# Two row norms moved into the output projections in front of them, with the projection's second half of columns taken by blocks of rows

## The chip, the cores and the metric

The kernel runs on one core of one Trainium2 chip. The metric is the device time of one execution in microseconds (us). A core has five engines with queues of their own: PE (TensorE, matrix products; "PEld" is its weight load), DVE (VectorE), ACT (ScalarE), POOL (GpSimd) and SP (SyncE, which here only issues transfers, DMAs). They are ordered among each other by semaphores alone.

## The reference

A block of one hybrid layer (a delta-rule branch and a sparse attention branch) is followed by two layers of a second model, the first with a dense feed-forward part and the second with eight experts. The sequence has 1024 tokens, the model width is 1024, everything is float32. What the change touches:

```
# end of the first block                      # layer 0 of the second block
y = concat([y_rwkv, y_attn]) @ w_out          x = x + concat([a, r]) @ w_out[0]
x = x + y                                     h = rmsnorm(x, ffn_norm[0])
x = rmsnorm(x, final_g)                       x = x + swiglu(h, dense weights)
                                              # layer 1: the same mix, then experts
rmsnorm(x, g) = x * rsqrt(mean(x*x, axis=-1) + 1e-6) * g
```

## The kernel before

The kernel is a sequence of stages. Each stage opens its own on-chip tiles and semaphores, runs one block of instructions per engine, and ends with `Stage.end`, which clears the semaphores and holds all engines at a barrier. So no work of one stage overlaps work of the next. Between stages activations are either on chip or in device memory: `x_block` (result of the first block), `x_mixed0` (after the mixing half of layer 0), `h_rows` (normed rows for the feed-forward part).

A float32 product is made of three products of rounded parts: a tile is rounded on ACT into a `high` part, DVE subtracts that from the tile for the `low` part, and PE adds high x high, high x low and low x high into one accumulator.

`product_rows` is the output projection, run three times (first block, layer 0, layer 1). Its operand is the transposed mix `lhsT`, 8 tiles (`k`) of 128 x 1024, its weights are 1024 x 1024. The outer loop is the half of the columns (`h`, 512 columns), then `k`, then the eight blocks `b` of 128 rows, one PSUM bank for each block. One step `n = 8h + k` loads one weight tile of 128 x 512 (256 KB, L1618), rounds operand tile and weight tile (ACT, L1657 and L1658), splits them (DVE, L1665 and L1666) and gives PE 24 products of 512 columns (L1639). All of these tiles have two buffers, so ACT rounds step n only when PE has finished step n-2, and the operand is rounded and split again in the second half. The residual rows come in two transfers of 2 MB (L1621), each issued on SP right behind a half's first weight tile. When a half's last `k` is done, DVE adds each bank to the residual (L1682). With `out` given (the two layers) SP then writes the rows (L1625).

`norm_rows` is the row norm in a stage of its own. The sequence is: all eight sums of squares on ACT (L1717, over 1024 columns), one mean for the eight blocks (DVE, L1725), one root (ACT, L1720), one reciprocal (DVE, L1727), eight scalings by root and gain (DVE, L1731), each written by SP (L1707), and then the wait for the last write. In the first block (`block_norm`) the rows are on chip from the projection. In layer 0 (`ffn_norm`, called by `dense_ffn`) they are read back from `x_mixed0` first (L1702). Behind `block_norm` stands `norm_transpose` of layer 0 (`mix_norm0`, its first load is L183), behind `ffn_norm` stands `swiglu_passes` (first weight load L2692 on SP, first rows `h_rows` on POOL, L2736).

## Time and profile before

| | |
|---|---|
| median of 3 runs | 5874.25 us (5873.77 to 5884.84) |
| the profiled execution, its own time | 5870.24 us |
| its span | 5868.6 us |
| PE busy | 5236.5 us (89% of the span) |
| DVE, ACT, POOL busy | 2812.8, 2150.8, 380.2 us (48%, 37%, 6%) |
| mean granted clock of PE | 0.94 of full speed |
| moved by DMA | 697.32 MB, 119 GB/s on average |

PE is the busiest engine in nearly every stretch of the run, so what a stage costs is mostly its products; where the row of PE has a hole, another engine or a transfer sets the time. A page of the profile gives busy shares for the whole run only. The time around the two norms has to be read from the timeline, engine by engine, since there PE does nothing at all and the stages are separated by barriers.

### The profile page before, as it was taken

How to read it: one execution, taken by the hardware profiler on the slowest of the kernel's cores; microseconds unless marked ns; L12 is line 12 of the kernel's file. 1: busy time of each engine (PE TensorE's matmuls, PEld its weight loads, DVE VectorE, ACT ScalarE, POOL GpSimd, SP SyncE). 2: the span in 40 equal slices, each digit the busy share in tenths (PEclk: the TensorE clock that was granted, in tenths of full speed). 3: DMA queues.
4: the chain of work that ended last, by engine and by line, in shares of the span. 5: the costliest groups of instructions: out<-in, count | busy, mean ns of one | idle time of the engine just before them, and what ended most of it. 6: DMA issues, size and time to landing. Idle time of an engine off the chain costs nothing. (4 is left out here: it accounts for less than half of the span.)

```text
span 5868.6 us, 96708 instructions
## 1 busy us (share of the span) xinstructions
PE 5236.5 (89%) x38308; PEld 4564.4 (78%) x38309; DVE 2812.8 (48%) x4375; ACT 2150.8 (37%) x3178; POOL 380.2 (6%) x577
## 2 busy tenths in 40 slices
PE   6984778969899599999799996999999999999994
PEld 5663776758776499999677775989898999999994
DVE  2598334451563355555228434444444555555444
ACT  2212114432344244444324432333333444444432
POOL 0113000000230000000005001000000000000001
PEclk8995999979999799999899996999999999999997
DMA  1110000031000555554210414444444455555544
GB/s 70 50 58 16 2 2 35 28 116 43 19 18 24 210 188 209 204 205 161 79 38 2 135 63 165 166 167 151 156 160 157 183 194 187 189 193 189 181 157 181
DMA packets 109898, 697.32 MB, mean 119 GB/s; under 512 B 12592, under 2 KB 16448, under 8 KB 68544
## 3 DMA queue, kind: packets, MB, share of 16 engines
q1 hardware_dynamic: 95744, 647.08, 30.5%
q0 software_dynamic: 9088, 28.48, 1.4%
q10 hardware_dynamic: 4800, 17.83, 0.8%
q8 instruction: 213, 3.49, 0.2%
q14 instruction: 53, 0.43, 0.0%
HBM read 631.06 MB, written 62.29 MB: 118 GB/s over the span
## 5 line engine op out<-in xcount | busy, mean ns | idle before, releaser
L3255 DVE TENSOR_TENSOR experts_low<-experts_raw,experts_high 128x1024 fp32r<-128x1024 f32 x678 | 810.7, 1224 | 1001.2 <-ACT experts_high L3184 1001.1
L3119 PE MATMUL ps<-experts_xs_high,experts_high 128*128 128x256 f32 (+1 forms) x3584 | 1038.2, 290 | 33.9 <-issue 32.5
L3119 PE MATMUL ps<-experts_xs_high,experts_low 128*128 128x256 f32 (+1 forms) x3584 | 1040.5, 290 | 0.0
L3119 PE MATMUL ps<-experts_xs_low,experts_high 128*128 128x256 f32 (+1 forms) x3584 | 1038.8, 290 | 0.0
L3119 PEld LDWEIGHTS ps<-experts_xs_high,experts_high 128*128 128x128 f32 x3584 | 680.3, 190 | 46.5 <-issue 37.1
L3184 ACT ACTIVATE experts_high<-experts_raw 128x1024 fp32r<-128x1024 f32 x678 | 687.8, 1049 | 36.6 <-DMA experts_raw<-experts 36.6
L3119 PEld LDWEIGHTS ps<-experts_xs_low,experts_high 128*128 128x128 f32 x3584 | 680.8, 190 | 9.1
L3119 PEld LDWEIGHTS ps<-experts_xs_high,experts_low 128*128 128x128 f32 x3584 | 680.8, 190 | 0.0
L2794 PE MATMUL ps<-dense_xs_parts,dense_high 128*128 128x256 f32 x2816 | 499.2, 280 | 4.2 <-DVE dense_xs_parts L2897 2.7
L2794 PEld LDWEIGHTS ps<-dense_xs_parts,dense_high 128*128 128x128 f32 x2816 | 436.6, 189 | 12.5 <-issue 5.0
L3111 PE MATMUL ps<-experts_high,experts_hid_high 128*128 128x512 f32 x1120 | 444.7, 397 | 0.0
L3111 PE MATMUL ps<-experts_low,experts_hid_high 128*128 128x512 f32 x1120 | 441.9, 395 | 0.0
L2794 PE MATMUL ps<-dense_xs_parts,dense_low 128*128 128x256 f32 x1408 | 393.7, 280 | 0.0
L3208 ACT ACTIVATE experts_silu<-ps 128x288 f32<-128x288 f32 (+1 forms) x224 | 89.1, 398 | 807.1 <-PE ps L3119 807.1
L2903 DVE TENSOR_TENSOR dense_low<-dense_raw,dense_high 128x1024 fp32r<-128x1024 f32 x270 | 323.3, 1222 | 65.3 <-ACT dense_high L2832 65.3
L3111 PE MATMUL ps<-experts_high,experts_hid_low 128*128 128x512 f32 x896 | 354.1, 395 | 0.0
L2832 ACT ACTIVATE dense_high<-dense_raw 128x1024 fp32r<-128x1024 f32 x270 | 283.8, 1054 | 55.9 <-PE ps L2779 22.4
L2794 PEld LDWEIGHTS ps<-dense_xs_parts,dense_low 128*128 128x128 f32 x1408 | 265.6, 189 | 0.0
L3214 ACT ACTIVATE experts_hid_high<-experts_hid 128x288 fp32r<-128x288 f32 (+1 forms) x224 | 96.6, 431 | 408.9 <-DVE experts_hid L3273 408.9
L3111 PEld LDWEIGHTS ps<-experts_low,experts_hid_high 128*128 128x128 f32 x1120 | 210.5, 188 | 39.9
L3111 PEld LDWEIGHTS ps<-experts_high,experts_hid_high 128*128 128x128 f32 x1120 | 210.4, 188 | 39.8
L3111 PEld LDWEIGHTS ps<-experts_high,experts_hid_low 128*128 128x128 f32 x896 | 168.3, 188 | 41.1
(547 smaller groups left out, 9144.1 us busy)
## 6 DMA issues: line engine op xcount, KB each, us to landing
experts_raw<-experts SPq DMA_DIRECT2D x226, 1536.0 KB, 6.3
dense_raw<-dense SPq DMA_DIRECT2D x90, 1536.0 KB, 6.3
mixT<-w_in SPq DMA_DIRECT2D x36, 512.0 KB, 3.2
y_slot<-mla_blank SPq DMA_DIRECT2D x15, 1152.0 KB, 20.7
out_proj_raw<-w_out SPq DMA_DIRECT2D x48, 256.0 KB, 2.7
proj_keys_raw<-w_in SPq DMA_DIRECT2D x20, 512.0 KB, 3.3
x_mixed<-x_out SPq DMA_DIRECT2D x16, 512.0 KB, 4.7
y_slot<-experts_y ACTq DMA_DIRECT2D x8, 1024.0 KB, 8.7
```

Source lines behind the costliest of these rows:

```text
L2794: last = nc.tensor.matmul(bank(u, m, SLOTS), w[:, u, m, c], x[:, k, :], start=(k == 0 and i == 0), stop=(k == KD - 1 and i == 2))
L2832: nc.scalar.activation(high[:, v, t, :], raw[:, v, t, :], ACT.Copy).then_inc(rounded, 1)
L2903: nc.vector.tensor_tensor(low[:, v, t, :], raw[:, v, t, :], high[:, v, t, :].bitcast(F32), ALU.subtract).then_inc(split, 1)
L3111: last = nc.tensor.matmul(ps[:, 2 + 2 * a + h, :], x, w[:, v, 2, c], start=first and i == 0, stop=last_one and i == len(terms) - 1)
L3119: last = nc.tensor.matmul(ps[:, m, 0:width], w[:, u, m, c], x[:, k, 0:width], start=(k == 0 and i == 0), stop=(k == KD - 1 and i == 2))
L3184: nc.scalar.activation(high[:, v, t, :], raw[:, v % NR, t, :], ACT.Copy).then_inc(rounded, 1)
L3208: nc.scalar.activation(silu[:, u % 2, 0:width], ps[:, 0, 0:width], ACT.Silu).then_inc(silu_done, 1)
L3214: nc.scalar.activation(hid_high[:, u % 2, 0:width], hid[:, u % 2, 0:width], ACT.Copy).then_inc(hid_rounded, 1)
L3255: nc.vector.tensor_tensor(low[:, v, t, :], raw[:, v % NR, t, :], high[:, v, t, :].bitcast(F32), ALU.subtract).then_inc(split, 1)
```

## The change

A new stage function, `product_and_norm`, takes the place of `product_rows` and `norm_rows` in the first block, and of `product_rows` in layer 0 together with `norm_rows` in `dense_ffn`. `norm_rows` is gone. Layer 1 keeps `product_rows`.

In the new stage the high and low parts of the operand (`x_high`, `x_low`) and of the weights have eight slots, one for each `k`. The operand is rounded and split once, in the first half. The first half of the columns runs as before, `k` outside and the eight blocks inside. During it the weight tiles of the second half are loaded and split into the slots that PE has finished with. The residual (and later the result) lies in the operand's own memory, so its one transfer of 4 MB waits until all eight operand tiles are split; SP issues it behind the tenth weight tile. The second half runs block by block: the 24 products of block 0, then of block 1, and so on, in the banks 0, 1 and 7 in turn. Behind each block's products DVE adds the bank to the rows, ACT sums the squares of the second half of the row (those of the first half were summed between the halves), DVE makes the mean, ACT the root, DVE the reciprocal and the scaled row, and SP writes it, while PE goes on with the next blocks. In layer 0 SP also writes the unscaled rows to `x_mixed0`, ahead of the scaled ones, and scaled rows have two buffers of their own. In the first block `masks` and in layer 0 `down` and `z` are released before the stage, which makes room.

```diff
--- before.py
+++ after.py
@@ -1683,53 +1683,142 @@
     st.end()
 
 
-def norm_rows(core, name, x, gain_row, out=None, source=None):
+def product_and_norm(core, name, xT, weights, source, gain_row, normed, out=None):
+
+
+
 
 
     nc = core.nc
     st = Stage(core, name)
-    junk = st.sb("junk", [P, D])
-    stat = st.sb("stat", [P, 3, NT])
+    K = 8
+    BANKS = (0, 1, 7)
+    x = as_rows(xT)
+    raw = st.sb("raw", [P, 2, HALF])
+    high = st.sb("high", [P, K, HALF], F32R)
+    low = st.sb("low", [P, K, HALF], F32R)
+    x_high = st.sb("x_high", [P, K, T], F32R)
+    x_low = st.sb("x_low", [P, K, T], F32R)
     gain = st.sb("gain", [P, D])
-    x_loaded = [st.sem(f"x_loaded{b}") for b in range(NT)]
-    loaded, summed, mean, root, inverse, normed, written = (
-        st.sem(n) for n in ("loaded", "summed", "mean", "root", "inverse", "normed", "written"))
+    junk = st.sb("junk", [P, HALF])
+    stat = st.sb("stat", [P, 6, NT])
+    rows = None if out is None else st.sb("rows", [P, 2, D])
+    row = lambda b: x[:, b, :] if out is None else rows[:, b % 2, :]
+    loaded = [st.sem(f"loaded{i}") for i in range(2)]
+    stored = [st.sem(f"stored{i}") for i in range(2)]
+    (xin, gain_in, rounded, split, used, product, added, summed, eased, mean, root, inverse, scaled, written) = (
+        st.sem(n) for n in ("xin", "gain_in", "rounded", "split", "used", "product", "added", "summed", "eased", "mean", "root",
+                            "inverse", "scaled", "written"))
     with nc.Block(name) as block:
         @block.sync
         def _(sp):
-            if source is not None:
+            for n in range(2 * K):
+                h, k = divmod(n, K)
+                if n >= 2:
+                    sp.wait_ge(split, n - 1)
+                sp.dma_start(raw[:, n % 2, :], weights[k * P:(k + 1) * P, h * HALF:(h + 1) * HALF]).then_inc(loaded[n % 2], 16)
+                if n == 1:
+                    sp.dma_start(gain[:, :], gain_row.to_broadcast([P, D])).then_inc(gain_in, 16)
+                if n == K + 1:
+                    sp.dma_start(x, source.rearrange("(b p) n -> p b n", p=P)).then_inc(xin, 16)
+            for b in range(NT):
+                if out is not None:
+                    sp.wait_ge(added, NT + b + 1)
+                    sp.dma_start(out[b * P:(b + 1) * P, :], x[:, b, :]).then_inc(written, 16)
+                sp.wait_ge(scaled, b + 1)
+                sp.dma_start(normed[b * P:(b + 1) * P, :], row(b)).then_inc(stored[b % 2], 16)
+            if out is not None:
+                sp.wait_ge(written, 16 * NT)
+            for i in range(2):
+                sp.wait_ge(stored[i], 16 * NT // 2)
+
+        @block.tensor
+        def _(pe):
+            def three(bank, k, b):
+                c = slice(b * P, (b + 1) * P)
+                nc.tensor.matmul(core.ps[:, bank, :], x_high[:, k, c], high[:, k, :], start=(k == 0), stop=False)
+                nc.tensor.matmul(core.ps[:, bank, :], x_high[:, k, c], low[:, k, :], start=False, stop=False)
+                return nc.tensor.matmul(core.ps[:, bank, :], x_low[:, k, c], high[:, k, :], start=False, stop=(k == K - 1))
+
+            for k in range(K):
+                pe.wait_ge(split, k + 1)
                 for b in range(NT):
-                    sp.dma_start(x[:, b, :], source[b * P:(b + 1) * P, :]).then_inc(x_loaded[b], 16)
-            sp.dma_start(gain[:, :], gain_row.to_broadcast([P, D])).then_inc(loaded, 16)
-            if out is not None:
-                for b in range(NT):
-                    sp.wait_ge(normed, b + 1)
-                    sp.dma_start(out[b * P:(b + 1) * P, :], x[:, b, :]).then_inc(written, 16)
-                sp.wait_ge(written, 16 * NT)
+                    last = three(b, k, b)
+                    if k == K - 1:
+                        last.then_inc(product, 1)
+                if k < K - 1:
+                    last.then_inc(used, 1)
+            for b in range(NT):
+                if b < 3:
+                    pe.wait_ge(added, BANKS[b] + 1)
+                else:
+                    pe.wait_ge(added, NT + b - 2)
+                for k in range(K):
+                    if b == 0:
+                        pe.wait_ge(split, K + k + 1)
+                    last = three(BANKS[b % 3], k, b)
+                last.then_inc(product, 1)
 
         @block.scalar
         def _(act):
+            def square(h, b):
+                act.wait_ge(added, h * NT + b + 1)
+                if h or b:
+                    act.wait_ge(summed, h * NT + b)
+                nc.scalar.activation(junk[:, :], x[:, b, h * HALF:(h + 1) * HALF], ACT.Square,
+                                     accum_out=stat[:, h, b:b + 1]).then_inc(summed, 1)
+
+            for n in range(2 * K):
+                h, k = divmod(n, K)
+                act.wait_ge(loaded[n % 2], 16 * (n // 2 + 1))
+                if h == 0:
+                    nc.scalar.activation(x_high[:, k, :], xT[:, k, :], ACT.Copy)
+                elif k < K - 1:
+                    act.wait_ge(used, k + 1)
+                else:
+                    act.wait_ge(product, NT)
+                nc.scalar.activation(high[:, k, :], raw[:, n % 2, :], ACT.Copy).then_inc(rounded, 1)
             for b in range(NT):
-                if source is not None:
-                    act.wait_ge(x_loaded[b], 16)
-                if b:
-                    act.wait_ge(summed, b)
-                nc.scalar.activation(junk[:, :], x[:, b, :], ACT.Square,
-                                     accum_out=stat[:, 0, b:b + 1]).then_inc(summed, 1)
-            act.wait_ge(mean, 1)
-            nc.scalar.activation(stat[:, 2, :], stat[:, 1, :], ACT.Sqrt).then_inc(root, 1)
+                square(0, b)
+            for b in range(NT):
+                square(1, b)
+                act.wait_ge(mean, b + 1)
+                nc.scalar.activation(stat[:, 4, b:b + 1], stat[:, 3, b:b + 1], ACT.Sqrt).then_inc(root, 1)
 
         @block.vector
         def _(dve):
+            def split_step(n):
+                dve.wait_ge(rounded, n + 1)
+                if n < K:
+                    nc.vector.tensor_tensor(x_low[:, n, :], xT[:, n, :], x_high[:, n, :].bitcast(F32), ALU.subtract)
+                nc.vector.tensor_tensor(low[:, n % K, :], raw[:, n % 2, :], high[:, n % K, :].bitcast(F32), ALU.subtract)\
+                    .then_inc(split, 1)
+
+            def add(h, b):
+                dve.wait_ge(product, h * NT + b + 1)
+                xs = x[:, b, h * HALF:(h + 1) * HALF]
+                nc.vector.tensor_tensor(xs, xs, core.ps[:, BANKS[b % 3] if h else b, :], ALU.add).then_inc(added, 1)
+            for n in range(2 * K - 1):
+                split_step(n)
+            dve.wait_ge(xin, 16)
+            for b in range(NT):
+                add(0, b)
+            split_step(2 * K - 1)
             dve.wait_ge(summed, NT)
-            nc.vector.tensor_scalar(stat[:, 1, :], stat[:, 0, :], 1.0 / D, 1e-6, ALU.mult, ALU.add).then_inc(mean, 1)
-            dve.wait_ge(root, 1)
-            nc.vector.reciprocal(stat[:, 0, :], stat[:, 2, :]).then_inc(inverse, 1)
-            dve.wait_ge(inverse, 1)
-            dve.wait_ge(loaded, 16)
+            nc.vector.tensor_scalar(stat[:, 2, :], stat[:, 0, :], 1.0 / D, 1e-6, ALU.mult, ALU.add).then_inc(eased, 1)
+            dve.wait_ge(eased, 1)
+            dve.wait_ge(gain_in, 16)
             for b in range(NT):
-                nc.vector.scalar_tensor_tensor(x[:, b, :], x[:, b, :], stat[:, 0, b:b + 1], gain[:, :],
-                                               ALU.mult, ALU.mult).then_inc(normed, 1)
+                add(1, b)
+                dve.wait_ge(summed, NT + b + 1)
+                nc.vector.scalar_tensor_tensor(stat[:, 3, b:b + 1], stat[:, 1, b:b + 1], 1.0 / D, stat[:, 2, b:b + 1], ALU.mult, ALU.add)\
+                    .then_inc(mean, 1)
+                dve.wait_ge(root, b + 1)
+                nc.vector.reciprocal(stat[:, 5, b:b + 1], stat[:, 4, b:b + 1]).then_inc(inverse, 1)
+                dve.wait_ge(inverse, b + 1)
+                if out is not None and b >= 2:
+                    dve.wait_ge(stored[b % 2], 16 * (b // 2))
+                nc.vector.scalar_tensor_tensor(row(b), x[:, b, :], stat[:, 5, b:b + 1], gain[:, :], ALU.mult, ALU.mult).then_inc(scaled, 1)
     st.end()
 
 
@@ -3390,8 +3479,6 @@
 def dense_ffn(core, source, out):
 
     nc, d = core.nc, core.dram
-    with nc.sbuf_tensor("ffn_x", [P, NT, D], F32) as x:
-        norm_rows(core, "ffn_norm", x, d["dense_g"], d["h_rows"], source)
     swiglu_passes(core, "dense", DFF // P, d["dense"], out, residual=source)
 
 
@@ -3421,8 +3508,8 @@
     with ExitStack() as s1:
         sb = lambda name, shape: s1.enter_context(nc.sbuf_tensor(f"{name}{l}", shape, F32))
         mixT = sb("mixT", [P, 8, T])
-        down = sb("down", [P, 6, T])
-        z = sb("z", [P, 4, T])
+        rest = s1.enter_context(ExitStack())
+        down, z = (rest.enter_context(nc.sbuf_tensor(f"{name}{l}", [P, n, T], F32)) for name, n in (("down", 6), ("z", 4)))
         with ExitStack() as s2:
             sb2 = lambda name, shape: s2.enter_context(nc.sbuf_tensor(f"{name}{l}", shape, F32))
             qk = sb2("qk", [P, 2, 4, T])
@@ -3453,8 +3540,12 @@
                                     (down[:, n, b * P:(b + 1) * P], key_rope[:, :])],
                       lambda n, j: values[:, j, n * P:(n + 1) * P],
                       lambda b: core.c("causal")[:, T - (b + 1) * P:T], 192 ** -0.5, mixT[:, 0:4, :], fill=l == 1)
+        rest.close()
         if dump:
             dump(core, f"mix{l}", mixT[:, :, :].rearrange("p a n -> p (a n)"))
+        if l == 0:
+            product_and_norm(core, f"out_proj{l}", mixT[:, :, :], d[f"w_out{l}"], source, d["dense_g"], d["h_rows"], out)
+            return
         x = sb("x_out", [P, NT, D])
         product_rows(core, f"out_proj{l}", mixT, 8, d[f"w_out{l}"], 2, x, source, out)
 
@@ -3466,9 +3557,9 @@
 
 def first_block(core, dump):
     nc, d = core.nc, core.dram
-    with nc.sbuf_tensor("masks", [P, offset(NT) - offset(TOPK // P)], F32) as masks:
-        with nc.sbuf_tensor("big", [P, 5, 4, T], F32) as big, nc.sbuf_tensor("small", [P, T], F32) as small:
-            flat = big[:, :, :, :].rearrange("p a j n -> p (a j) n")
+    with nc.sbuf_tensor("big", [P, 5, 4, T], F32) as big:
+        flat = big[:, :, :, :].rearrange("p a j n -> p (a j) n")
+        with nc.sbuf_tensor("masks", [P, offset(NT) - offset(TOPK // P)], F32) as masks, nc.sbuf_tensor("small", [P, T], F32) as small:
             down, queries, relu = flat[:, 0:4, :], flat[:, 8:10, :], flat[:, 10:12, :]
             with nc.sbuf_tensor("index_weight", [P, NT, IDX_HEADS], F32) as weight, ExitStack() as s2:
                 xT = split_tensors(core, s2, "xT", [P, KD, T])
@@ -3502,13 +3593,11 @@
                     pair_products(core, "values_up", lambda n: flat[:, 4 + n, :],
                                   [[(w_uv[:, 2 * r, :], o_lat[:, 2 * r, :]), (w_uv[:, 2 * r + 1, :], o_lat[:, 2 * r + 1, :])]
                                    for r in range(4)], gate=lambda n: space[:, n, :])
-            if dump:
-                dump(core, "mixT", flat[:, 0:8, :].rearrange("p a n -> p (a n)"))
-            with nc.sbuf_tensor("x_res", [P, NT, D], F32) as x:
-                product_rows(core, "out_proj", flat[:, 0:8, :], 8, d["w_out"], 2, x, d["x"])
-                norm_rows(core, "block_norm", x, d["final_g"], d["x_block"])
-                if dump:
-                    dump(core, "x1", x[:, :, :].rearrange("p a n -> p (a n)"))
+        if dump:
+            dump(core, "mixT", flat[:, 0:8, :].rearrange("p a n -> p (a n)"))
+        product_and_norm(core, "out_proj", flat[:, 0:8, :], d["w_out"], d["x"], d["final_g"], d["x_block"])
+        if dump:
+            dump(core, "x1", flat[:, 0:8, :].rearrange("p a n -> p (a n)"))
 
 
 def index_weights(core, small, weight):
```

## Rows read from the trace of the kernel before

**Rows 1.** The page's first part: busy time and share of the span of each engine.
```profile
PE 5236.5 (89%) x38308; PEld 4564.4 (78%) x38309; DVE 2812.8 (48%) x4375; ACT 2150.8 (37%) x3178; POOL 380.2 (6%) x577
```

**Rows 2.** Timeline of PE behind both norms: start, us, instructions [idle before <-releaser].
```profile
1273.93 5.01 PE L270 MATMUL ps<-cst,mixT 128*128 128x128 f32 x24 [36.33 <-DVE mixT L235]
...
2036.00 1.97 PE L2761 MATMUL ps<-cst,dense_xs 128*128 128x128 f32 x8 [54.49 <-DMA dense_xs<-h_rows]
```

**Rows 3.** Timeline of DVE, ACT and SP from the first block's projection to the next stage.
```profile
1232.96 5.37 DVE L1682 TENSOR_TENSOR x_res<-x_res,ps 128x512 f32<-128x512 f32 x8 [2.70 <-PE ps L1639]
...
1248.50 1.28 ACT L1720 ACT_TABLE_LOAD   x1
...
1250.27 9.66 DVE L1731 SCALAR_TENSOR_TENSOR x_res<-x_res,block_norm_stat,block_norm_gain 128x1024 f32<-128x1024 f32 x8
...
1264.18 0.32 SPq L183 DMA_DIRECT2D qk<-x_block  x1
```

**Rows 4.** The same from layer 0's projection to the dense stage.
```profile
1976.86 5.37 DVE L1682 TENSOR_TENSOR x_out<-x_out,ps 128x512 f32<-128x512 f32 x8 [2.70 <-PE ps L1639]
...
2005.84 9.66 DVE L1731 SCALAR_TENSOR_TENSOR ffn_x<-ffn_x,ffn_norm_stat,ffn_norm_gain 128x1024 f32<-128x1024 f32 x8
...
2019.72 37.97 SPq L2692 DMA_DIRECT2D dense_raw<-dense  x7
```

**Rows 5.** Instructions on single tiles: duration in ns min/median/max, first and last start.
```profile
L1682 DVE TENSOR_TENSOR x_res<-x_res,ps x16: 679/684/689, 1191.5 to 1237.6; 128x512 f32<-128x512 f32 x16
L1731 DVE SCALAR_TENSOR_TENSOR x_res<-x_res,block_norm_stat,block_norm_gain x8: 1280/1281/1285, 1250.3 to 1258.6; 128x1024 f32<-128x1024 f32 x8
L1658 ACT ACTIVATE out_proj_high<-out_proj_raw x48: 612/613/617, 1145.1 to 3514.1; 128x512 fp32r<-128x512 f32 x48
```

**Rows 6.** Timeline of ACT and DVE in `norm_transpose`, where squares and roots alternate.
```profile
1272.17 0.19 ACT L203 ACTIVATE mix_norm_stat<-mix_norm_stat 128x1 f32<-128x1 f32 x1
1272.38 1.06 ACT L199 ACTIVATE mixT<-qk 128x1024 f32<-128x1024 f32 x1
1273.35 0.19 ACT L199 ACTIVATION_READ_ACCUMULATOR mixT<-qk 128x1 f32 x1
1273.44 0.19 ACT L203 ACTIVATE mix_norm_stat<-mix_norm_stat 128x1 f32<-128x1 f32 x1
...
1272.30 0.15 DVE L223 TENSOR_SCALAR mix_norm_stat<-mix_norm_stat 128x1 f32<-128x1 f32 x1 [3.25 <-ACT mixT L199]
1272.39 0.17 DVE L227 RECIPROCAL mix_norm_stat<-mix_norm_stat 128x1 f32<-128x1 f32 x1
```

**Rows 7.** Timeline of ACT: two successive steps, each released by PE's products.
```profile
1205.06 1.06 ACT L1657 ACTIVATE out_proj_x_high<-big 128x1024 fp32r<-128x1024 f32 x1 [3.86 <-PE ps L1639]
1210.50 1.06 ACT L1657 ACTIVATE out_proj_x_high<-big 128x1024 fp32r<-128x1024 f32 x1 [3.86 <-PE ps L1639]
```

**Rows 8.** Timeline of PE between the two halves of the first block's projection.
```profile
1192.88 0.39 PE L1639 MATMUL ps<-out_proj_low,out_proj_x_high 128*128 128x512 f32 x1
1193.11 0.39 PE L1639 MATMUL ps<-out_proj_high,out_proj_x_low 128*128 128x512 f32 x1
1193.80 0.47 PE L1639 MATMUL ps<-out_proj_high,out_proj_x_high 128*128 128x512 f32 x1 [0.30 <-PE ps L1639]
```

**Rows 9.** Timeline of PE: products at the lower clock, then from one bank to the next at the higher.
```profile
1149.04 0.63 PE L1639 MATMUL ps<-out_proj_high,out_proj_x_high 128*128 128x512 f32 x1
1149.46 0.63 PE L1639 MATMUL ps<-out_proj_low,out_proj_x_high 128*128 128x512 f32 x1
...
1152.99 0.39 PE L1639 MATMUL ps<-out_proj_high,out_proj_x_low 128*128 128x512 f32 x1
1153.21 0.39 PE L1639 MATMUL ps<-out_proj_high,out_proj_x_high 128*128 128x512 f32 x1
```

**Rows 10.** DMA issues of the first block's projection: count, KB each, median us to landing.
```profile
out_proj_raw<-w_out SPq DMA_DIRECT2D x16, 256.0 KB, 2.6
x_res<-x SPq DMA_DIRECT2D x2, 2048.0 KB, 8.4
```

## The prediction

> **What bounds the kernel now.** I read the page's first part first: PE is busy 89% of the span, no other engine over half of it [rows 1]. So a change elsewhere pays only where PE has a hole. The timeline of PE shows two at the norms: 36.33 us idle ahead of the first transpose of layer 0, and 54.49 us ahead of the first of the dense stage [rows 2]. Next I read the other engines across those holes. In the first, DVE's last add runs to 1238.33, then eight squares, a table load and a root pass on ACT, the eight scalings end at 1259.93, and the next stage issues its first load at 1264.18 [rows 3]. The second holds the same and a trip through memory: the adds end at 1982.23, the scalings at 2015.50, the next stage starts at 2019.72 [rows 4]. The work of ACT and DVE in these holes is serial and under no product. The rest of each hole (from 1264.18, from 2019.72) belongs to the next stage, and the change leaves it alone.
>
> **Removed: the serial norm.** I count from the start of the last add, which directly follows the last product, to the next stage's first transfer. The last add starts 0.68 before the adds' end: 1237.65 and 1981.55 [rows 3 to 5]. Before, the stretches are 1264.18 - 1237.65 = 26.53 us and 2019.72 - 1981.55 = 38.17 us.
>
> **Added: the last block's chain.** Only block 7 has nothing to hide under. Its parts: add 0.68 [rows 5]; square of 512 columns, priced as the 512-column copy of 0.61 plus the accumulator read 0.19 less their overlap 0.09 (1.06 + 0.19 take 1.16 from 1272.38 to 1273.54 on [rows 6]), so 0.71 [rows 5, 6]; mean, priced as the 0.15 to 0.17 of the small DVE operations, 0.17; root 0.19; reciprocal 0.17 [rows 6]; scaling 1.28 [rows 5]; five handoffs between engines, an estimate of 0.03 each, 0.15 (the rows show no visible pause between mean and reciprocal on DVE [rows 6]; at 0.1 each it would be 0.5). That is 3.35. From the end of the last scaling to the next stage's first transfer, which holds the last write, its landing, the clearing and the barrier, it was 1264.18 - 1259.93 = 4.25 and 2019.72 - 2015.50 = 4.22 [rows 3, 4], and stays. In layer 0 the write of the unscaled rows of the same block goes out some 2.7 us ahead of the scaled ones on the same queue; I give it 0.3 (between 0 and the 1.3 by which a block of 512 KB would last at the rate of the 2 MB transfer below). The new stretches are 7.60 and 7.87, the gains 18.93 and 30.30 us, together 49.2.
>
> **Added under the products.** Two successive ACT steps start 5.44 us apart, each waiting for PE's 24 products [rows 7]: 0.227 us a product, and so 5.44 us for a block of rows too. The chain of a block is the 3.35 above, and DVE's share of it 2.3. It fits with 2.1 us to spare, so blocks 0 to 6 and the squares of the first half cost nothing; without that cover they would cost 8 x 3.35. With three banks PE is three blocks ahead of what it needs freed. The table load of 1.28 [rows 3] moves to the first root, at block 0, where PE has two blocks in hand: nothing. Rounding and splitting the operand once instead of twice frees ACT and DVE, which PE did not wait for in the middle of a half: nothing.
>
> **Moved: the boundary of the halves.** Before, the product after the last of the first half starts 0.69 later instead of 0.227 [rows 8], because the counting of finished banks drains PE. Block order needs bank 0 alone, added long before. That takes 0.46 away twice, 0.9 (0 if PE drains there all the same).
>
> **Moved: the 4 MB transfer.** SP issues it behind weight tile 9, that is when split 8 is done; the weight tiles 10 to 15 queue behind it. A 256 KB tile lands in 2.6 us, 2 MB in 8.4 [rows 10]. By the difference, 5.8 us for 1792 KB, the second 2 MB cost 6.6, so 4 MB land after 15.0 us; twice 8.4, 16.8, is the upper bound, and 13.7 the lower (the whole of the 2.6 taken as latency that the 2 MB hide but once, so 5.3 for the second 2 MB). With two raw buffers a pair of steps takes a landing of 2.6, ACT's 1.6 and DVE's 1.85, about 6.1, so split 8 comes some 20.5 us after the first split. PE needs 8 x 5.44 = 43.5 for the first half. All from the first split: the transfer is issued at 20.9 and lands at 35.9, tile 10 0.6 later. Its rounding and split (0.61 + 0.68) are done at 37.9, and only then is tile 12 issued: 2.6 + 1.4 more to split 13 at 41.9, and again to split 15 at 45.9. PE, whose first ten products are slow, ends the first half at 7.7 + 7 x 5.44 = 45.8. DVE's order is split 15, then the eight adds, then split 16. So bank 0, which PE wants at 45.8, is added at 46.6: a wait of 0.8 a stage where there was none, and behind DVE's wait for the transfer and for the splits queue all the adds. The last split ends the eight adds (4.9) and 0.7 later, at 51.5, and is wanted 21 products (4.8) into block 0, at 51.4: the same lateness, not a second one. I take 0.8 a stage, 1.6 for both (bounds 0 and 2.6 a stage, by 13.7 and 16.8 us of transfer).
>
> **Same-bank products.** 24 products in a row now add to one bank. From one product to the next it is 0.23 us within a bank [rows 8] and 0.22 into another [rows 9]; the order costs nothing.
>
> **The sum.** 49.2 + 0.9 - 1.6 = 48.5 us, under the profiled execution's own 5870.24: 5821.7 (span 5820.1). That execution lies 4.0 under the median of the runs, so on the scale of the median it is 5874.25 - 48.5 = 5825.8. I forecast 5826.
>
> **Rivals.** (a) The 4 MB transfer holds up the splits, the adds and so PE at the boundary by its upper bound or more: 2.6 a stage in place of 0.8, 5830. For it speaks that there is no margin, against it that full rows are contiguous pieces twice as long as those of the 8.4 us transfer.
>
> (b) ACT changes tables for each block, square to root and back. Two loads of 1.28 make the chain 5.95 us, over PE's 5.44: 7 x 0.5 late plus 2.6 in the last block, 6.2 a stage, 5838. Against it: in `norm_transpose` root, square and root follow each other with no load between [rows 6].
> The Trainium skill ("ScalarE: Activation LUTs", Table sets: the hidden batching unit, and What ACT_TABLE_LOAD costs) says that a change between sets is paid each time, about 2.66 us with a drain, and does not name square among what the root's set holds. By that figure the chain would be 8.7 us and the estimate 28 a stage, 5882, no gain at all; the same section counts cheap functions as part of every set, and rows 6 put square among them.
>
> (c) The other side: PE's granted clock. The second half now has PE wait on a bank's release at each of eight blocks. At its lower level (1.2 GHz) a product takes 0.425 us instead of 0.227 [rows 9]. Both second halves, 384 products, would take 76 us more: 5902, slower than before. It turns into a loss once two thirds of these products run low (48.5 of 76). Against it: before, PE waited for a bank in front of every three products at the start of the second half and no slow product followed [rows 8]; and the wait is met in advance by two blocks.
> The Trainium skill ("TensorE: Matmul & The Clock Gate", A second HAM failure mode: psum-queue depth-cycling) describes just this, banks cycled with small idle pieces between groups and a clock that oscillates. By it this case would be likely; the rows, which show no idle piece to come, make it a small chance.
>
> (d) The change does what it says and the next stages give some back or add some: PE starts them after a shorter hole, its clock rises at another product, and all later holes shift. The first product of a stage starts at the lower level for some ten products at 0.2 us each [rows 9], 2 us either way for each stage touched, 5818 to 5834.
>
> **How the numbers follow.** Forecast 5826 (with its own 5820 to 5831): 0.66. (a) 0.14, (b) 0.03 including the dearer switch, (c) 0.02, (d) beyond the forecast's own range 0.15, evenly to both sides. The range of 8 in 10 is 5814 to 5838: below it a gain of 60 us, which needs the scatter of the execution against the median (4 us) and (d) together; above it (a) and (d) together. 0.2% is 11.7 us, about what a measurement can tell from no change. Faster by more than that holds in the forecast, (a), (d) and the cheap form of (b): 0.96. Within 0.2%: 0.01. Slower: (c) and a rest, 0.03.
>
> **What would show it.** Right: the last scaling ends about 3.4 us after the last product of each new stage and the next stage's first transfer follows 4.2 later; the holes of PE fall to 36.3 - 18.9 = 17.4 and 54.5 - 30.3 = 24.2 us; one table load a stage; products 5.44 us a block, and at the boundary a hole of about 0.8 us ahead of block 0. Wrong: an idle piece of PE at the boundary of over 2 us, released by DVE's split or add (a), a table load between square and root in each block (b), a granted clock under 1 in the second half (c), or holes of the expected length and a time that isn't, with more slow products in later stages (d).

## The result, and the profile after

The changed kernel takes 5816.05 us, the median of 4 runs (5808.69 to 5819.51), against 5876.69 (5873.77 to 5884.84, 4 runs) for the kernel before, measured beside it: a ratio of 0.9898 with a 95% interval of 0.9886 to 0.991, 60.6 us less. The profiled execution took 5808.69 us, its span is 5807.1. One of the eleven executions of "places only" below took 13974.63 us, more than twice the others, and is left out everywhere.

The page's first part, after (it answers to [rows 1]):

```profile
span 5807.1 us, 96706 instructions
...
PE 5230.5 (90%) x38308; PEld 4560.4 (79%) x38309; DVE 2799.8 (48%) x4389; ACT 2142.7 (37%) x3208; POOL 381.5 (7%) x577
```

PE has the same 38308 products and nearly the same busy time (5236.5 before). So 55.5 of the 61.5 us between the spans are idle time of PE that is gone, and the timeline of PE behind the two stages has most of it (it answers to [rows 2]):

```profile
1250.24 2.18 PE L270 MATMUL ps<-cst,mixT 128*128 128x128 f32 x9 [16.73 <-DVE mixT L235]
...
1980.37 1.97 PE L2850 MATMUL ps<-cst,dense_xs 128*128 128x128 f32 x8 [22.96 <-DMA dense_xs<-h_rows]
```

The holes are 16.73 and 22.96 us instead of 36.33 and 54.49, 51.1 us less together. What is left in the first can be followed through the timeline of DVE, ACT and SP for the last block of rows (it answers to [rows 3]; columns as there):

```profile
1138.61 0.80 SPq L1719 DMA_DIRECT2D out_proj_raw<-w_out  x2
...
1198.74 1.28 ACT L1786 ACT_TABLE_LOAD   x1
...
1228.11 0.69 DVE L1800 TENSOR_TENSOR big<-big,ps 128x512 f32<-128x512 f32 x1 [2.05 <-PE ps L1741]
...
1233.55 0.69 DVE L1800 TENSOR_TENSOR big<-big,ps 128x512 f32<-128x512 f32 x1 [2.05 <-PE ps L1741]
1234.27 0.63 ACT L1768 ACTIVATE out_proj_junk<-big 128x512 f32<-128x512 f32 x1 [4.29 <-DVE big L1800]
1234.80 0.19 ACT L1768 ACTIVATION_READ_ACCUMULATOR out_proj_junk<-big 128x1 f32 x1
1235.02 0.16 DVE L1814 SCALAR_TENSOR_TENSOR out_proj_stat<-out_proj_stat 128x1 f32<-128x1 f32 x1 [0.79 <-ACT out_proj_junk L1768]
1235.22 0.20 ACT L1786 ACTIVATE out_proj_stat<-out_proj_stat 128x1 f32<-128x1 f32 x1 [0.23 <-DVE out_proj_stat L1814]
1235.45 0.16 DVE L1817 RECIPROCAL out_proj_stat<-out_proj_stat 128x1 f32<-128x1 f32 x1 [0.27 <-ACT out_proj_stat L1786]
1235.65 1.28 DVE L1821 SCALAR_TENSOR_TENSOR big<-big,out_proj_stat,out_proj_gain 128x1024 f32<-128x1024 f32 x1
...
1240.52 0.32 SPq L183 DMA_DIRECT2D qk<-x_block  x1
```

Two adds start 5.44 us apart, and DVE is idle for 2.05 us of each such period ahead of the add, waiting for PE: the norm of a block of rows fits under the products of the next. From the last add's start to the scaling's end it is 1236.93 - 1233.55 = 3.38 us, and 3.59 more to the next stage's first transfer. The 26.53 us of [rows 3] are 6.97. The one table load lies at the first block. In layer 0 the same stretch, 38.17 us in [rows 4], is 1964.43 - 1957.44 = 6.99:

```profile
1860.42 0.80 SPq L1719 DMA_DIRECT2D out_proj_raw<-w_out  x2
...
1957.44 0.69 DVE L1800 TENSOR_TENSOR mixT<-mixT,ps 128x512 f32<-128x512 f32 x1 [2.05 <-PE ps L1741]
...
1964.43 28.32 SPq L2781 DMA_DIRECT2D dense_raw<-dense  x6
```

The measure used from here on is the length of a stage: from SP's first transfer of the projection to SP's first transfer of the next stage (so with the norm's stage where there is one). Before, these lengths are 1264.18 - 1141.45 = 122.7 us and 2019.72 - 1884.74 = 135.0 us. After, they are 1240.52 - 1138.61 = 101.9 and 1964.43 - 1860.42 = 104.0. So 20.8 + 31.0 = 51.8 us of the 61.5 lie in the changed stages. Of the other 9.7, 2.8 lie ahead of the first of them, 5.6 behind layer 1's projection, where the stage of the experts is the longest, and the rest in small pieces; all of this is code that the change doesn't touch. Whether these 9.7 us belong to the change at all is the question of the last experiments.

The second thing that could have gone wrong is the start of the second half. The timeline of DVE and PE there, first in the first block's stage, then in layer 0's:

```profile
1187.18 0.69 DVE L1794 TENSOR_TENSOR out_proj_low<-out_proj_raw,out_proj_high 128x512 fp32r<-128x512 f32 x1 [2.47 <-ACT out_proj_high L1780]
1187.79 4.86 DVE L1800 TENSOR_TENSOR big<-big,ps 128x512 f32<-128x512 f32 x8
...
1912.80 4.86 DVE L1800 TENSOR_TENSOR mixT<-mixT,ps 128x512 f32<-128x512 f32 x8
...
1912.36 0.39 PE L1741 MATMUL ps<-out_proj_high,out_proj_x_low 128*128 128x512 f32 x1
1913.54 0.50 PE L1739 MATMUL ps<-out_proj_high,out_proj_x_high 128*128 128x512 f32 x1 [0.79 <-DVE mixT L1800]
```

The two transfers of the residual in the view of DMAs (count, KB, us from issue to landing; they answer to [rows 10]):

```profile
big<-x SPq DMA_DIRECT2D x1, 4096.0 KB, 13.1
...
mixT<-x_block SPq DMA_DIRECT2D x1, 4096.0 KB, 14.3
```

In layer 0 the transfer lands after 14.3 us, DVE's split of step 15 ends late, and PE waits 0.79 us for bank 0. In the first block the transfer lands after 13.1 us and PE does not wait at all; there the products of the second half follow those of the first 0.23 us apart, as within a half. The two later profiles of the changed kernel have waits of 1.10 and 0.57 us in layer 0 and again none in the first block.

### The profile page after: what moved, and what is told of

It reads as the page before. It is cut to its first block and busy times, and to the rows that moved or that the text cites. A ratio compares the mean times of both kernels' runs of the same rounds, so it can differ in the third digit from the quotient of the medians.

```text
span 5807.1 us, 96706 instructions
## 1 busy us (share of the span) xinstructions
PE 5230.5 (90%) x38308; PEld 4560.4 (79%) x38309; DVE 2799.8 (48%) x4389; ACT 2142.7 (37%) x3208; POOL 381.5 (7%) x577
## 5 line engine op out<-in xcount | busy, mean ns | idle before, releaser
L3208 PE MATMUL ps<-experts_xs_high,experts_high 128*128 128x256 f32 (+1 forms) x3584 | 1038.6, 290 | 30.0 <-issue 28.7
```

The source lines that it names most:

```text
L3208: last = nc.tensor.matmul(ps[:, m, 0:width], w[:, u, m, c], x[:, k, 0:width], start=(k == 0 and i == 0), stop=(k == KD - 1 and i == 2))
```

## The experiments

Every kernel is the changed one with one edit unless it says otherwise. The lengths of the three projection stages (first block, layer 0, and layer 1, which the change leaves as it was) stand beside the medians, since they are free of what happens elsewhere. They come from one profile each; between profiles of one kernel they differ by up to 0.9 us. "One bank", "two tables" and "copy ahead" were executed once, so for them only the stages count.

| kernel | median us (runs) | kernel before, beside it | ratio, 95% interval | first block | layer 0 | layer 1 |
|---|---|---|---|---|---|---|
| before | 5876.69 (4) | | | 122.7 | 135.0 | 106.2 |
| after | 5816.05 (4) | 5876.69 | 0.9898 (0.9886 to 0.991) | 101.9 | 104.0 | 105.8 |
| after, second set | 5821.88 (4) | 5879.9 | 0.9902 (0.9887 to 0.9917) | 101.9 | 104.5 | 105.8 |
| after, third set | 5823.09 (5) | 5874.61 | 0.9914 (0.99 to 0.9928) | 102.8 | 104.3 | 105.6 |
| before, second profile | 5880.99 (11) | 5883.25 | 0.9997 (0.9988 to 1.0006) | 122.1 | 135.7 | 106.2 |
| first block only | 5856.41 (5) | 5879.9 | 0.9957 (0.9944 to 0.9971) | 102.8 | 136.1 | 106.3 |
| layer 0 only | 5852.99 (5) | 5879.9 | 0.9951 (0.9937 to 0.9964) | 121.8 | 104.9 | 105.8 |
| places only | 5879.25 (10) | 5879.9 | 1.0 (0.9991 to 1.0009) | 122.9 | 135.8 | 106.2 |
| k outside | 5862.82 (9) | 5883.02 | 0.997 (0.996 to 0.9981) | 122.2 | 123.9 | 105.8 |
| one bank | 5839.67 (1) | 5883.02 | | 112.2 | 112.8 | 105.7 |
| two tables | 5847.3 (1) | 5883.02 | | 109.0 | 109.9 | 105.7 |
| copy ahead | 5851.6 (1) | 5883.02 | | 116.6 | 118.2 | 105.7 |
| rows on ACT's queue, layer 1 by blocks | 5818.64 (4) | 5874.61 | 0.9907 (0.9891 to 0.9922) | 102.6 | 103.3 | 100.9 |
| after with pads | 5880.6 (11) | 5874.61 | 1.0007 (0.9997 to 1.0016) | 125.1 | 140.0 | 106.1 |

### One norm at a time, and the places of the tiles alone

Theory: each stage gains for itself what its norm took. Rivals: part of the 60 us comes from where tiles lie on chip (the change releases and opens some at other points), or from a stage that starts at another time. "First block only" restores layer 0, "layer 0 only" restores the first block, "places only" restores both but keeps the new points at which tiles are opened and released.

```diff
 # first block only (norm_rows is put back as it was)
-        if l == 0:
-            product_and_norm(core, f"out_proj{l}", mixT[:, :, :], ..., d["dense_g"], d["h_rows"], out)
-            return
 # dense_ffn
+    with nc.sbuf_tensor("ffn_x", [P, NT, D], F32) as x:
+        norm_rows(core, "ffn_norm", x, d["dense_g"], d["h_rows"], source)
 # places only, in addition
-        product_and_norm(core, "out_proj", flat[:, 0:8, :], d["w_out"], d["x"], d["final_g"], d["x_block"])
+        with nc.sbuf_tensor("x_res", [P, NT, D], F32) as x:
+            product_rows(core, "out_proj", flat[:, 0:8, :], 8, d["w_out"], 2, x, d["x"])
+            norm_rows(core, "block_norm", x, d["final_g"], d["x_block"])
```

> Only the first block has the new stage; layer 0 keeps product_rows and norm_rows. Theory A (stage sum): gain 20.8 us, a time of about 5856 beside 5877. Theory B (placement of tiles in the first block, with masks behind big): up to 29 us, since all of the surplus would come with this part.

> Only layer 0 has the new stage; the first block is as before, with its own placement of tiles. Theory A: gain 31 us, a time of about 5846 beside 5877. Theory B: 31 too, with nothing gained ahead of 1140 us. A rival C, that an earlier start of the expert stage is what shortens it: 36.

> All stages as before; only the tiles are opened and released where the changed kernel does it (masks opened after big and released before the first block's projection, down and z of both layers released before the projection). Theory A: no change, within 3 us of before. Theory B: 3 to 9 us faster, with rwkv_output_and_queries some 3 us shorter in the profile.

The changed kernel ran beside them once more:

> The changed kernel once more, unaltered, to see how much of its gain is fixed. In the first pair of profiles the two changed stages account for 20.8 and 31.0 us (51.8), the medians differ by 60.6, and the profiles by 61.5, of which 2.8 lie ahead of the first changed stage and 5.5 in the expert stage, in code that is the same. Theory A (what lies outside the two stages is scatter of the granted clock's phase): over more runs the gain comes to 52, between 49 and 56, and the expert stage lasts about as long as before (2335 us). Theory B (the moved tiles or the shifted start make untouched stages faster each time): the gain stays at 60 and the expert stage stays near 2330 us in every profile.

Measured: the first block alone gives 23.5 us (its stage 20 shorter), layer 0 alone 26.9 us (its stage 30 to 31 shorter), the places of the tiles nothing (5879.25 against 5879.9), and the changed kernel repeated 58.0 (5821.88 against 5879.9; stages 101.9 and 104.5). In the stages the gain is the sum of two that don't depend on each other: 20 and 30 to 31 alone, 20.8 and 31.0 together. The whole times don't add up as well: 23.5 and 26.9 make 50.4, not 58.0, and layer 0 alone, expected at 5846, came to 5852.99, a gain 4 us below that of its stage. The rival of the places falls.

### Order of the second half: k outside again

Theory: the norm is hidden by the order by blocks of rows, not by the merging of the stages or by the operand split only once. The edit keeps all of these and puts `k` outside again in the second half, with eight banks:

```diff
-            for b in range(NT):
-                ...
-                for k in range(K):
-                    ...
-                    last = three(BANKS[b % 3], k, b)
-                last.then_inc(product, 1)
+            for k in range(K):
+                pe.wait_ge(split, K + k + 1)
+                for b in range(NT):
+                    if k == 0:
+                        pe.wait_ge(added, b + 1)
+                    last = three(b, k, b)
+                    if k == K - 1:
+                        last.then_inc(product, 1)
 # and DVE adds bank b instead of BANKS[b % 3]
```

> As the changed kernel, norm inside the stage, but the second half runs k outside and the eight blocks inside, in eight banks, as before the change. Theory A (the order by blocks is what hides the norm): DVE's order is add, mean, reciprocal, scaling for each block in turn, 3.38 us a block by the changed kernel's timeline, so eight of them, 27 us, start 4.8 before the last product and end 22 behind it, instead of 3.4: each of the two stages 19 us longer (101.9 to 121, 104.0 to 123), 38 in all, 5858 to 5862. Rival (sparing the barriers, the read back and the serial squares is what brings the gain, whatever the order): no more than 5 us a stage longer.

Measured: the stages are 122.2 and 123.9 us, 20.3 and 19.9 longer than after. The timeline of DVE and SP of this kernel, from the last product on:

```profile
1235.91 0.69 DVE L1798 TENSOR_TENSOR big<-big,ps 128x512 f32<-128x512 f32 x1 [31.65 <-PE ps L1741]
...
1240.30 0.68 DVE L1798 TENSOR_TENSOR big<-big,ps 128x512 f32<-128x512 f32 x1
...
1243.60 0.68 DVE L1798 TENSOR_TENSOR big<-big,ps 128x512 f32<-128x512 f32 x1
...
1262.20 1.28 DVE L1819 SCALAR_TENSOR_TENSOR big<-big,out_proj_stat,out_proj_gain 128x1024 f32<-128x1024 f32 x1
...
1267.07 0.32 SPq L183 DMA_DIRECT2D qk<-x_block  x1
```

DVE stands for 31.65 us while PE makes the products of all blocks, and then the eight chains come one behind the other, 3.30 us each. So the chain of one block that the changed kernel shows (3.38) is about what each of the seven hidden ones costs when there is nothing over it. Against the kernel before the merged stage without the order by blocks gains next to nothing in the first block (122.2 to 122.7) and 11 us in layer 0 (123.9 to 135.0), where the trip through memory falls away. The order is worth about 20 us a stage, 40 of the 52; the other 12 come with the merging, nearly all of them in layer 0.

### One bank for all blocks: rival (c), idle pieces of PE and its clock

The changed kernel has no idle piece of PE inside the second half, so it can't tell what such pieces do. With a single bank PE must wait for each block's add:

```diff
-                if b < 3:
-                    pe.wait_ge(added, BANKS[b] + 1)
-                else:
-                    pe.wait_ge(added, NT + b - 2)
+                if b < 1:
+                    pe.wait_ge(added, 1)
+                else:
+                    pe.wait_ge(added, NT + b)
                 ...
-                    last = three(BANKS[b % 3], k, b)
+                    last = three(0, k, b)
 # and DVE adds bank 0 in the second half
```

> As the changed kernel, but all eight blocks of the second half in bank 0, so that PE waits for DVE's add before each block. Theory A (a pause, the clock stays): seven pauses of 0.8 us, each stage 5.6 us longer, 11 in all, granted clock 1.00 in the second half. Rival (the pauses between groups make the clock oscillate, as the Trainium skill, TensorE: Matmul & The Clock Gate, A second HAM failure mode: psum-queue depth-cycling, says): slow products at 0.425 us among those at 0.227 in the second halves, up to 38 us more a stage.

The timeline of PE at the starts of blocks 1, 2 and 3, and then the windows of the second half (stretch, length, busy time and count of PE, PEld, DVE, ACT and POOL, granted clock, DMA share, GB/s):

```profile
1200.51 0.50 PE L1739 MATMUL ps<-out_proj_high,out_proj_x_high 128*128 128x512 f32 x1 [2.59 <-DVE big L1800]
...
1207.06 0.50 PE L1739 MATMUL ps<-out_proj_high,out_proj_x_high 128*128 128x512 f32 x1 [0.78 <-DVE big L1800]
...
1213.58 0.50 PE L1739 MATMUL ps<-out_proj_high,out_proj_x_high 128*128 128x512 f32 x1 [0.78 <-DVE big L1800]
...
1197.00:1243.00 46.00, 38.73 (x164) 29.78 (x163) 16.24 (x29) 10.02 (x29) 0.00 (x0) 1.00 0.17 69
```

The clock stays at 1.00, 2.4 GHz, in spite of a pause ahead of each block from the second on; so does it in the changed kernel, which has none:

```profile
1189.00:1233.00 44.00, 44.00 (x196) 36.46 (x195) 20.39 (x37) 14.07 (x39) 0.00 (x0) 1.00 0.20 79
```

The stages grew by 10.3 and 8.8 us, more than the 5.6 of the expectation, for two reasons. A pause costs more than its 0.78: blocks start 6.52 us apart instead of 5.44, 1.08 more. The first product after it is shown with 0.50 instead of 0.39; that it and its weight load overlap nothing before them is the likely reason, and no run isolates it. And the first pause is 2.59 (2.02 in layer 0), since on DVE the add of block 0 is queued behind the wait for all squares of the first half (it starts at 1199.77, right behind DVE's wait of 3.98 us for ACT's squares). The rival of the clock is not borne out: pauses of 0.8 us every 6.5 us do not lower it here. The Trainium skill ("TensorE: Matmul & The Clock Gate", A second HAM failure mode: psum-queue depth-cycling) describes such pauses at bank changes with an oscillating clock. This trace doesn't agree: in windows of 46 us over the second halves of "one bank" the granted clock is 1.00 in both stages.

### Two tables a block: rival (b)

The changed kernel loads the root's table once a stage. To see what a change in each block would have cost, an exponential was put between square and root, whose result nobody uses:

```diff
                 square(1, b)
+                nc.scalar.activation(stat[:, 6, b:b + 1], stat[:, 0, b:b + 1], ACT.Exp, scale=0.0)
                 act.wait_ge(mean, b + 1)
```

> As the changed kernel, with one small Exp on ACT (its result is not used) between square and root of each block, so that the table is changed twice a block. By the rows (a load of 1.28 us and nothing else): the block's chain grows by 1.28 + 0.2 + 1.28 - 0.2 to about 6.0 us, over PE's 5.44, so 7 x 0.55 + 2.6 = 6.5 us a stage, 13 in all. By the page's figure (2.66 us a change, with a drain): the chain is 8.7, 28 us a stage, 56 in all, and nothing of the gain is left.

The timeline of ACT in the last two blocks of the first stage:

```profile
1232.66 1.28 ACT L1785 ACT_TABLE_LOAD   x1
1233.95 0.20 ACT L1785 ACTIVATE out_proj_stat<-out_proj_stat 128x1 f32<-128x1 f32 x1
1234.16 1.28 ACT L1787 ACT_TABLE_LOAD   x1
1235.45 0.20 ACT L1787 ACTIVATE out_proj_stat<-out_proj_stat 128x1 f32<-128x1 f32 x1
...
1237.80 0.63 ACT L1768 ACTIVATE out_proj_junk<-big 128x512 f32<-128x512 f32 x1 [2.15 <-DVE big L1801]
```

Load, function, load, function start 1.29, 0.21 and 1.29 us apart: a change of tables costs its 1.28 and nothing beside it. The stages grew by 7.1 and 5.9 us, 6.5 expected. The Trainium skill ("ScalarE: Activation LUTs", What ACT_TABLE_LOAD costs) adds a drain of about 1.38 us to every switch to another set; this trace shows none (the load's own 1.28 us agrees), and an effect of 28 us a stage, which followed from that figure, did not come either. So rival (b) was rightly priced by the rows, and it fell because square and root alternate without a load, one load a stage in the changed kernel.

### A copy ahead of the 4 MB transfer: rival (a)

Here SP first issues a copy of 4 MB from memory to memory that nobody reads, on the same queue directly ahead of the residual's transfer, so that this one lands late:

```diff
                 if n == K + 1:
+                    sp.dma_start(core.dram["x_ffn"], source).then_inc(copied, 16)
                     sp.dma_start(x, source.rearrange("(b p) n -> p b n", p=P)).then_inc(xin, 16)
 ...
+            sp.wait_ge(copied, 16)
```

> As the changed kernel, with a copy of 4 MB from memory to memory (into x_ffn, which is free at the time) issued on SP right ahead of the 4 MB of residual rows. Theory A (the weight tiles behind it wait, and the boundary has a margin of 1.4 us in the first block and none in layer 0): if the copy lasts D, PE stands still at the boundary for D - 1.4 and D + 0.8, with D between 10 (the rate of the residual's transfer) and 26 us (both directions paid). Rival (a transfer on the queue does not hold up the later ones by its whole length, they share the engines): much less than D, and tile 10 lands well before the residual rows do.

The two landings in the view of DMAs:

```profile
big<-x SPq DMA_DIRECT2D x1, 4096.0 KB, 25.1
...
mixT<-x_block SPq DMA_DIRECT2D x1, 4096.0 KB, 25.8
```

PE's timeline at the start of the second half in either stage:

```profile
1206.39 0.80 PE L1742 MATMUL ps<-out_proj_high,out_proj_x_high 128*128 128x512 f32 x1 [10.77 <-DVE big L1803]
...
1946.18 0.80 PE L1742 MATMUL ps<-out_proj_high,out_proj_x_high 128*128 128x512 f32 x1 [13.37 <-DVE mixT L1803]
1946.77 0.63 PE L1743 MATMUL ps<-out_proj_low,out_proj_x_high 128*128 128x512 f32 x1
```

A landing later by 12.0 and 11.5 us made pauses of 10.77 and 13.37 us. So the transfer is on the path nearly one for one from the point at which the changed kernel has it: in layer 0 there is no reserve at all (0.79 of wait already; 11.5 later make 12.6 more), in the first block about 1.2 us (12.0 less 10.8). The stages grew by 14.7 and 14.2 us, in the first block 3.9 and in layer 0 1.6 more than the added pause (10.8; 13.4 less the 0.8 that was there). A pause of this length costs the clock as well, other than the short ones above. The windows from the last products of the first half to some 7 us into the second:

```profile
1190.00:1209.00 19.00, 8.23 (x31) 6.45 (x30) 6.66 (x11) 6.04 (x13) 0.00 (x0) 0.73 0.50 181
1209.00:1216.00 7.00, 7.00 (x25) 5.57 (x25) 2.98 (x6) 3.66 (x11) 0.00 (x0) 0.76 0.00 1
```

The granted clock falls to a mean of 0.73 and 0.76, and twelve products behind the pause's first are shown with 0.63 instead of 0.39, as at the start of a stage [rows 9]. From 1206.39 to 1212.11 thirteen products start, in 5.72 us instead of 2.95: 2.8 of the 3.9 us. The rest stays open.

### A version that goes on from there

If the order by blocks pays without a norm too, layer 1's projection should take it, since its eight adds lie behind its last product. And if the 4 MB transfer holds up the weight tiles on its own queue, another queue should free them. Both edits together:

```diff
 # sync: the residual's transfer is gone from here; scalar:
                 nc.scalar.activation(high[:, k, :], raw[:, n % 2, :], ACT.Copy).then_inc(rounded, 1)
+                if n == K:
+                    act.wait_ge(split, K)
+                    act.dma_start(x, source.rearrange("(b p) n -> p b n", p=P)).then_inc(xin, 16)
 # layer 1, with all steps of the norm left out where gain_row is None
-        product_rows(core, f"out_proj{l}", mixT, 8, d[f"w_out{l}"], 2, x, source, out)
+        product_and_norm(core, f"out_proj{l}", mixT[:, :, :], d[f"w_out{l}"], source, None, None, out)
```

> The changed kernel with two steps more: the 4 MB of residual rows go out on ACT's queue instead of SP's, so that the weight tiles don't stand behind them, and layer 1's projection uses the new stage too, with no norm in it (rows are only added and written, by blocks). Stage sum: the residual's queue takes the 0.8 us pause of PE in layer 0 away and changes nothing in the first block, where there was none; in layer 1 the stretch from the last add to the next stage's first transfer falls from 9.0 to 0.7 + 3.6 = 4.3 us, with 0.5 at the boundary. Layer 1's stage 105.8 to 100.6, layer 0's 104.2 to 103.4, 6 us in all under the changed kernel: 5813 beside 5819 to 5822. Rival: both queues share the same engines, so the weight tiles land no earlier (tile 10 still 13 us behind), and layer 0 stays at 104.2.

The timeline of DVE and SP at the end of layer 1's projection:

```profile
3470.86 0.69 DVE L1803 TENSOR_TENSOR mixT<-mixT,ps 128x512 f32<-128x512 f32 x1 [4.75 <-PE ps L1741]
...
3475.09 0.33 SPq L181 DMA_DIRECT2D moe_router<-router  x1
```

Layer 0's residual in the view of DMAs:

```profile
mixT<-x_block ACTq DMA_DIRECT2D x1, 4096.0 KB, 16.6
```

The last add of layer 1 and the next stage's first transfer start 4.23 us apart, 9.0 before; the stage went from 106.2 to 100.9. In layer 0 the transfer now takes 16.6 us but holds up no weight tile by its whole length (DVE's longest wait between splits is 5.8 us instead of 11.8), PE's wait at the boundary is gone, and the stage is 103.3 instead of 104.0. The three stages together are some 5 us shorter than after. The whole time, 5818.64, misses the 5813 of the expectation and can't be told from that of the changed kernel (5816.05 to 5823.09 in its three sets, 5823.09 in the one beside it): by its stages the version is the shorter one, and the total doesn't show it.

### The 7 us outside the stages

Pooled over all executions, 72 of the kernel before have a mean of 5879.7 us (standard deviation 5.9) and 13 of the changed kernel 5820.3 (6.4): 59.4 us. The stages hold 51.8, so that some 7 or 8 us seem to lie in code that the change doesn't touch. Theories: (1) it hangs on when the later stages start; (2) it belongs to the compiled kernel as a whole, whatever the starts; (3) scatter.

The pooled number is weaker than it looks. The executions come in sets on several chips, and the median of the kernel before differs from set to set, from 5874.61 to 5883.25, by more than the scatter within a set explains (standard error of a set of 15: 1.1 to 1.5). So each set of the changed kernel is to be compared with the kernel before beside it alone:

| set of the changed kernel | gain, difference of the means (standard error) | gain of the two stages | rest |
|---|---|---|---|
| first | 62.9 (3.5) | 51.8 | 11.1 |
| second | 56.9 (2.9) | 51.3 | 5.6 |
| third | 51.2 (3.3) | 50.7 | 0.5 |

The rest is 5.7 us in the mean of the three, with a standard error of 3.1 from their scatter, and in the third set it is 0.5. Other kernels miss their stages to both sides: "layer 0 only" gained 26.4 us in the means where its two stages hold 31.0, "k outside" 18.4 where they hold 11.6. So a lasting surplus is not shown. For (1), two pads bring the starts of the changed kernel back to about those of before: copies of 6 and of 9.9 MB from memory to memory that nobody reads, ahead of layer 0 and ahead of the dense stage.

```diff
 # ahead of layer 0
+            load(core, "pad_a", [(dram["x_ffn"], dram["x"]), (dram["x_mixed1"][0:512, :], dram["x"][0:512, :])])
 # ahead of the dense stage
+    load(core, "pad_b", [(d["x_ffn"], d["x"]), (d["x_mixed1"], d["x"]), (d["y_slot"][0:480, :], d["x"][0:480, :])])
```

> The changed kernel with what it saved put back as idle time: memory-to-memory copies in stages of their own, about 19 us ahead of layer 0 and about 33 us ahead of the dense stage (nobody uses the copies), sized so that all later stages start about when they did before the change. The question is the surplus of 6 to 9 us over the 52 us of the two stages. If it comes from an earlier start of the later stages (theory C), the time without the pads is that of the kernel before without its two norms, some 7 us longer than that of the changed kernel without pads. If it is scatter of the clock's phase or sits in the stages themselves, the untouched stages last as long as in the changed kernel.

The changed kernel and the one before once more:

> The changed kernel a third time, unaltered, beside more runs of the kernel before: stage sum 52 us of gain, theory of a lasting surplus 58 to 60.

> The kernel before the change, unaltered, for a second profile of it. Over the runs so far the means of the kernel before and of the changed one lie 58 us apart, of which the two stages hold 51.5; the pads, put in a third kernel, cost what they last, so the start of later stages is not what makes the rest. If the rest is the clock's scatter in the expert stage, this profile's stages outside the two projections and norms come to anything between 5601 and 5627 us, as in the other kernels; if a lasting difference in one untouched stage makes it, that stage is again longer here than in all three profiles of the changed kernel (expert stage over 2198, with the rest the same). The two changed stretches should again be 122.7 and 135.5 us, within 1.

The pads lengthen the two stages by 22.3 and 35.7 us against the third profile of the changed kernel, 58.1 together, so that layer 0 and the dense stage start at 1268.85 and 2033.36 us, 5 and 14 later than before the change. The padded kernel has a mean of 5878.9 us, 55.7 (standard error 3.9) over that of the changed kernel beside it: it pays for its pads and no more. With (1) it would have paid some 7 more, 65, so the run speaks against (1), but only by about 2.4 standard errors, and in this set there was no surplus to explain.

The profiles say much the same. The code outside the two stages took 5610.9 us in the first profile of the kernel before and 5618.6 in the second (within the 5601 to 5627 of its expectation), and 5601.2, 5607.9 and 5610.4 us in those of the changed kernel. The changed kernel is lower in the mean, by 8, but its third profile and the first of the kernel before are equal, and two profiles of one kernel lie 8 to 9 apart. Behind layer 1's projection alone it is 2335.7 and 2340.5 against 2330.1, 2334.2 and 2335.0 us, lower in all three of the changed kernel, but by as little as 0.7. Scatter, (3), is not excluded by this, nor is a small lasting difference.

Where such a difference lies, as that of the first pair, shows best in the stage of the experts, the longest. Its window in the kernel before (columns as above):

```profile
3610.00:5808.00 2198.00, 2127.30 (x14104) 1975.83 (x14104) 1038.94 (x1306) 876.24 (x1200) 57.71 (x69) 0.98 0.47 171
```

The same in the changed kernel:

```profile
3555.00:5747.00 2192.00, 2127.34 (x14104) 1976.14 (x14104) 1038.84 (x1306) 876.30 (x1200) 57.40 (x69) 0.98 0.47 172
```

Most of the difference of 6 us (3.8) stands in PE's largest group of waits in this window (tile and line, releaser: idle us, count, longest). Before, first profile:

```profile
PE ps L3119 <- issue: 32.5, 7, 9.9
```

"Places only":

```profile
PE ps L3258 <- issue: 42.7, 13, 10.1
```

After:

```profile
PE ps L3208 <- issue: 28.7, 7, 7.9
```

"One bank":

```profile
PE ps L3208 <- issue: 38.9, 14, 10.1
```

All engines have the same busy time within 0.4 us; what differs is idle time of PE put down to "issue", in which the engine waited for nothing that the profile shows. It comes in 7 to 14 pieces of up to 10 us. It is 32.5 and 37.4 us in two executions of the kernel before, 28.7, 28.5 and 30.2 in three of the changed one, 31.3 in the padded one, 29.9 in the version with ACT's queue, and between 33.7 and 42.7 in all the others, also in those that have both new stages ("one bank" 38.9). That would fit (2), an effect of the whole compiled kernel that happens to favour this one, and scatter nearly as well, since the two executions of the kernel before differ by 4.9 and its first is within 1.2 of the padded kernel. It is a correlation over these kernels; no run took the cause away or put it back, and the cause stays open.

## Why the prediction was right

Predicted were 5826 us (5814 to 5838) and 48.5 us of gain; it took 5816.05, 60.6 less, and 5821.88 and 5823.09 when repeated. The range holds all three. The changed stages gave 51.8 of it (51.3 and 50.7 in the repeats), 3.3 more than predicted, and by them alone the time would have been 5876.69 - 51.8 = 5824.9. The other 8.8 us of the first set come from nothing that the prediction argued, and they brought its time within 2 us of the range's lower end; that it stayed inside is luck. Step by step:

- **The serial norm goes.** Right in both places and in size: of the 26.53 us stay 6.97 and of the 38.17 stay 6.99 (7.60 and 7.87 predicted). Holes of PE of 17.4 and 24.2 us were expected, 16.73 and 22.96 came. That the order by blocks does this, and no other part, is shown by "k outside".
- **The last block's chain.** 3.35 predicted, 3.38 measured; added up from single rows of other stages, it held to 1%.
- **The end of the stage.** Mis-sized: it was taken over as 4.25 and 4.22, and the 0.3 for the second write added. It measured 3.59 and 3.60. Before, eight writes of 512 KB went out 1.2 us apart and the last one queued behind the others (3.0 us to landing in the median); now they are 5.44 apart (2.6). This part is argued from the medians, no run isolated it; "k outside", where the writes go out 3.30 us apart, has the same 3.59. It is 0.7 and 0.9 us of extra gain.
- **Seven chains under the products, for nothing.** Right: blocks 5.44 us apart, DVE idle 2.05 in each. "K outside" puts their price without cover at 3.30 each, and "two tables" shows where the cover ends: at a chain of 5.89 the block's period is no longer 5.44.
- **The boundary and the 4 MB transfer.** The time to the landing was mis-sized, 15.0 against 13.1 and 14.3, and below the lower bound of 13.7 in the first block. That bound does not follow from its own words either: 8.4 less 2.6 is 5.8, not 5.3, so it would be 14.2, farther still from 13.1. In layer 0 the transfer went out 21.8 us after the first split instead of 20.9, so that it landed at 36.1, as good as the predicted 35.9: the wait of 0.79 (1.10 and 0.57 in the repeats) is the predicted 0.8 in part because two misses cancel. In the first block it went out at 20.3, landed at 33.4, and PE did not wait: 0.8 us more gain. The remark that there is no margin was right: "copy ahead" turned 11.5 us of delay into 12.6 of wait in layer 0.
- **The drain between the halves.** Right in the first block, where the 0.46 us are gone. In layer 0 the wait covers it: from the last product of the first half to the first of the second it is 1.18 us.
- **The first stage's slow products.** Seven instead of ten at its start, 0.6 us, the kind of thing that rival (d) had. It is scatter and not the change: the second profile of the kernel before has six, the third of the changed kernel ten.

With these the first block's stage comes to 18.9 + 0.5 + 0.6 (chain and end) + 0.6 (slow products) = 20.6 of the 20.8 measured, layer 0's to 30.3 + 0.5 - 0.8 + 0.9 = 30.9 of 31.0.

- **Rivals.** (a) The transfer never reached its upper bound, though it decides from there on. (b) One table load a stage; two a block would have cost 6 to 7 us a stage. (c) The clock stayed at 1.00 in both second halves. (d) It had the time go either way by slow products at the starts of later stages, 5818 to 5834. A shift in untouched stages did come in the first profile, beyond that range in the first set of runs and inside it in the two repeats, but mostly as idle "issue" time of PE in a stage over a millisecond later, and it is not shown to be the change's.

## What to carry to other kernels

A reduction over rows behind a product is hidden when the product's last part is ordered by rows rather than by the inner dimension: then each block's chain (here 3.4 us) has the next block's products (5.4 us) over it, and only the last one shows. The condition in this kernel is that all parts of both operands fit on chip for that part, and the place to look for the new bound is the transfer that has to fill the space which they held. When a sum over stages and the whole time differ by a tenth of the gain, compare the stages, and repeat the pair before claiming the rest for the change: here the rest was 11.1, 5.6 and 0.5 us in three sets, and pooling over sets would have hidden that.
